# Gated delta stage: another order in its prologue, rotary angles moved into its last head, last head's output on VectorE

## The reference, cut to what matters

```python
def gdn_mixer(h, w_in, w_conv, a_log, dt_bias, w_onorm, w_out):
    proj = h @ w_in
    qkv, z, beta_logit, a_logit = split(proj)          # 3 x 1024, 1024, 8, 8 columns
    qkv = silu(causal_conv(qkv, w_conv))               # 4 taps along the tokens
    q, k, v = heads(qkv)
    q = q * rsqrt(sum(q * q) + EPS) / sqrt(d)
    k = k * rsqrt(sum(k * k) + EPS)
    beta = sigmoid(beta_logit)
    g = -exp(a_log) * softplus(a_logit + dt_bias)
    o = chunk_gated_delta(q, k, v, g, beta)            # running sums of g, state over the blocks
    o = o * rsqrt(mean(o * o) + EPS) * w_onorm
    return (o * silu(z)) @ w_out

x = x + gdn_mixer(rms_norm(x, norm_w[2]), ...)
x = x + swa_mixer(rms_norm(x, norm_w[3]), positions, ...)
#   swa_mixer rotates q and k by cos/sin of  positions[..., None] * inv_freq
```

## Time and profile before

| | |
|---|---|
| median of 3 runs | 3170.13 us (3170.04 to 3171.9) |
| profiled execution: its own time | 3169.11 us |
| profiled execution: its span | 3167.1 us |
| busy in the span: PE, DVE, ACT, POOL | 2859.8, 1312.1, 1210.2, 978.9 us |
| mean granted TensorE clock | 0.962 of full speed |
| prologue of gdn, from cb's last matmul to head 0's first | 592.1 to 632.0 us |
| gdn heads | 632.0 to 1000.9 us |
| output product of gdn, from the held parts to the last sum | 1008.9 to 1049.4 us |

### The profile page before, as it was taken

The page is one execution under the profiler, slowest core; times in us unless marked ns, Lnnn a source line. Parts: engine busy times, 40 slices in busy tenths (PEclk is TensorE's granted clock), DMA queues, the critical chain, the costliest instruction groups (busy, mean ns, idle before and its releaser), DMA issues.

```text
span 3167.1 us, 41439 instructions
## 1 busy us (share of the span) xinstructions
PE 2859.8 (90%) x13752; PEld 2148.3 (68%) x13752; DVE 1312.1 (41%) x2370; ACT 1210.2 (38%) x1832; POOL 978.9 (31%) x420
## 2 busy tenths in 40 slices
PE   6999999799998799788888999997799999899996
PEld 5777777567766577566676888875445646688875
DVE  2234223676675565555534122125543343411131
ACT  4333333344443354444443233344333333432233
POOL 3443332222232323222222444432111212344433
PEclk9999999899999899899999999999899999999998
DMA  4232221211111212211122333221100102233322
GB/s 137 92 93 79 67 66 53 67 54 39 41 53 37 70 60 63 64 53 53 54 62 64 102 97 98 94 87 56 40 27 27 60 26 60 67 93 100 93 80 67
DMA packets 59505, 213.35 MB, mean 67 GB/s; under 512 B 6560, under 2 KB 6944, under 8 KB 59296
## 3 DMA queue, kind: packets, MB, share of 16 engines
q1 hardware_dynamic: 57920, 208.46, 21.5%
q0 software_dynamic: 528, 2.10, 0.2%
q10 hardware_dynamic: 976, 1.70, 0.2%
HBM read 210.14 MB, written 2.10 MB: 67 GB/s over the span
## 4 chain that ended last, share of the span: by engine, by line
issue 53%; PE 24%; POOL 15%; DVE 6%; ACT 1%; POOLq 0%; DVEq 0%; ACTq 0%; PEldq 0%
POOL weights_low L342 15%; PE bank L386 4%; PE bank L387 4%; PE bank L388 4%; PE bank L986 3%; PE bank L988 2%; PE bank L987 2%; DVE work L1438 1%; PE bank L1083 1%; DVE work L1435 1%; DVE mixed L1945 1%; PE bank L449 0%; PE bank L1067 0%; DVE residual L1949 0%; DVE work L1508 0%
## 5 line engine op out<-in xcount | busy, mean ns | idle before, releaser
L342 POOL TENSOR_TENSOR weights_low<-weights_raw,weights_high 128x1024 fp32r<-128x1024 f32 x391 | 946.8, 2424 | 2002.7 <-ACT weights_high L335 2002.6
L386 PE MATMUL bank<-activations_high,weights_high 128*128 128x512 f32 x1848 | 729.4, 395 | 23.5 <-DVEq L2669 6.4
L387 PE MATMUL bank<-activations_low,weights_high 128*128 128x512 f32 x1848 | 721.5, 390 | 0.0
L388 PE MATMUL bank<-activations_high,weights_low 128*128 128x512 f32 x1848 | 720.9, 390 | 0.0
L986 PE MATMUL bank<-activations_high,weights_high 128*128 128x512 f32 x1232 | 534.6, 434 | 49.6 <-DVE activations_low L416 42.6
L335 ACT ACTIVATE weights_high<-weights_raw 128x1024 fp32r<-128x1024 f32 x391 | 412.1, 1054 | 352.8 <-PE bank L388 270.4
L988 PE MATMUL bank<-activations_high,weights_low 128*128 128x512 f32 x1232 | 493.1, 400 | 0.0
L987 PE MATMUL bank<-activations_low,weights_high 128*128 128x512 f32 x1232 | 493.0, 400 | 0.0
L386 PEld LDWEIGHTS bank<-activations_high,weights_high 128*128 128x128 f32 x1848 | 348.3, 188 | 109.0 <-issue 22.6
L387 PEld LDWEIGHTS bank<-activations_low,weights_high 128*128 128x128 f32 x1848 | 348.2, 188 | 74.8 <-issue 3.4
L388 PEld LDWEIGHTS bank<-activations_high,weights_low 128*128 128x128 f32 x1848 | 348.1, 188 | 73.3
(11 more groups left out here) (380 smaller groups left out, 3121.9 us busy)
## 6 DMA issues: line engine op xcount, KB each, us to landing
weights_raw<-weights SPq DMA_DIRECT2D x391, 512.0 KB, 3.6
residual<-x_t POOLq DMA_DIRECT2D x1, 2048.0 KB, 16.2
out_t<-residual SPq DMA_DIRECT2D x1, 2048.0 KB, 7.1
const<-consts SPq DMA_DIRECT2D x1, 1033.5 KB, 4.9
work<-p_t ACTq DMA_DIRECT2D x2, 512.0 KB, 3.6
work<-positions ACTq DMA_DIRECT2D x1, 256.0 KB, 3.2
root<-positions ACTq DMA_DIRECT2D x1, 256.0 KB, 3.0
param<-params SPq DMA_DIRECT2D x1, 140.5 KB, 5.0
```

Of the source, the lines that this page charges most:

```text
L342: K.nc.gpsimd.tensor_tensor(K.w_lo[:, s, :], K.raw[:, s, :], K.w_hi[:, s, :].bitcast(F32), ALU.subtract).then_inc(K.job_sems["low"], 1)
L386: K.nc.tensor.matmul(dst, wh, K.act_hi[:, t, :], start=first, stop=False)
L387: K.nc.tensor.matmul(dst, wh, K.act_lo[:, t, :], start=False, stop=False)
L388: ins = K.nc.tensor.matmul(dst, wl, K.act_hi[:, t, :], start=False, stop=last)
```

## The change

The diff has three parts.

1. Prologue. DVE's clearing moves ahead of the normalization (`gdn_cleared` tells ACT that the gates' buffer is clear). Beta is made by ACT as exp(-ln(1 + exp(-x))) and DVE's reciprocal goes. ACT's table load and `fetch` calls move between the gate steps, and the convolutions of q and k are woven into DVE's gate steps. PE does 3 parts of c0+2, the transposes, the other 5 parts, and puts 4 parts of c0+3 behind each `norm_sum`; it waits for `gdn_begin` after them. The weight splits of c0+3 to c0+5 move with them on ACT, and so on POOL.
2. Angles. The positions are loaded into `K.root` before the last head (`fetch_positions` on ACT's queue), and `rope_angles` takes the place of the empty generator in DVE's last head. The output product then uses the looped `out_residual_dve` without them. The sines stay where they were.
3. Last head's output. DVE does the three operations that POOL did, for the last head alone.

```diff
@@ gdn_pe
-    for r in range(1, 3):
-        job(e, c0 + r)
+    job(e, c0 + 1)
+    values = job_parts(e, c0 + 2)
+    take(values, 3)
     e.eng.wait_ge(K.sem("gdn_gates"), 1)
...
     ins.then_inc(K.sem("gdn_gates_t"), 1)
-    e.eng.wait_ge(K.sem("gdn_begin"), 1)
+    take(values, DT)
...
+    gate = job_parts(e, c0 + 3)
     for part in range(2):
         norm_sum(part, 0, c0 + part)
-    job(e, c0 + 3)
+        take(gate, 4)
+    e.eng.wait_ge(K.sem("gdn_begin"), 1)
@@ gdn_act   (the old gate steps and the loop of fetches are removed)
+    weight_high(e, cb + AHEAD)
+    nc.scalar.preload_act_table_set("natural_log_exp_and_others")
+    st.step(act(b.ea[32:40, 0:1], K.col("gdn_a_log", 0)[32:40, :], ACT.Exp))
+    job_wait(e, cb)
+    beta = b.gates[0:H8, :]
+    e.eng.wait_ge(K.sem("gdn_cleared"), 1)
+    step(act(beta, bank_of(e, cb)[0:H8, :], ACT.Exp, scale=-1.0))
+    step(act(beta, beta, ACT.Ln, bias=one[0:H8, :]))
+    act(beta, beta, ACT.Exp, scale=-1.0).then_inc(K.sem("gdn_beta"), 1)
+    fetch(0)
+    e.eng.wait_ge(K.sem("gdn_dt"), 1)
+    step(act(b.eg[32:40, :], b.eg[32:40, :], ACT.Exp))
+    act(b.eg[32:40, :], b.eg[32:40, :], ACT.Ln, bias=one[32:40, :]).then_inc(K.sem("gdn_ln"), 1)
+    weight_high(e, c0 + AHEAD)
+    fetch(1)
+    e.eng.wait_ge(K.sem("gdn_gates"), 1)
+    act(b.eg[32:40, :], b.bg[32:40, :], ACT.Exp).then_inc(K.sem("gdn_eg"), 1)
+    e.eng.wait_ge(K.sem("gdn_tok_in"), 1)
+    act(b.f1, b.tok[:, :, 32:40], ACT.Exp).then_inc(K.sem("gdn_f1_e"), 1)
+    weight_high(e, c0 + 1 + AHEAD)
+    silu(0)
+    fetch(2)
+    weight_high(e, c0 + 2 + AHEAD)
+    silu(1)
     roots()
...
+    fetch_positions(e, K.positions, 0)
     head(H8 - 1, False, False)
@@ gdn_pool
             weight_low(e, c0 + 3 + AHEAD + r, i)
+        if not more:
+            return
@@ gdn_dve
+    (memsets of u, sf, row2, tmp and gates, then sem_inc gdn_cleared)
     prenorm_dve(e, "gdn", "norm_w", 2 * DT, cb)
...
+    first = convolutions(0, (0, 1))
+    job_wait(e, cb)
+    (three steps on x, the second of them to gdn_dt)
+    e.eng.wait_ge(K.sem("gdn_beta"), 1)
+    release(e, cb)
+    st.step(v.memset(b.row1.bitcast(F32), 0.0))
+    take(first, 4)
+    e.eng.wait_ge(K.sem("gdn_ln"), 1)
+    (add, scale, running sum, copy to gdn_gates; three copies of rows)
+    e.eng.wait_ge(K.sem("gdn_gates_t"), 1)
+    v.tensor_copy(b.tok, by_chunk(K.ps[4][:, 0:NG * CH])).then_inc(K.sem("gdn_tok_in"), 1)
+    take(first, 4)
+    (two subtractions; after gdn_eg two copies and a subtraction; after gdn_f1_e the product f1)
     select(0)
-    take(convolutions(0, (0, 1)), 8)
     normalize()
...
-        conv_v, conv = convolutions(i, (2,)), convolutions(i + 1, (0, 1)) if more else iter(())
+        conv_v, conv = convolutions(i, (2,)), convolutions(i + 1, (0, 1)) if more else swa_angles(e)
...
+    e.eng.sem_inc(K.sem("position_room"), 1)
     head(H8 - 1, False)
+    last, split = H8 - 1, FIRST_SPLIT["gdn_y"] + H8
+    e.eng.wait_ge(K.sem("gdn_o_rstd"), H8)
+    e.eng.wait_ge(K.sem("gdn_o_free"), H8 + 1)
+    step(v.tensor_tensor(b.o, b.o, b.r, ALU.mult))
+    e.eng.wait_ge(K.sem("gdn_z"), H8)
+    v.tensor_tensor(b.o, b.o, b.z, ALU.mult).then_inc(K.sem("y_done"), 1)
+    e.eng.wait_ge(K.sem("split_high_done"), split)
+    v.tensor_tensor(K.act_lo[:, last + DT, :], b.o, K.act_hi[:, last + DT, :].bitcast(F32),
+                    ALU.subtract).then_inc(K.sem("split_done"), 1)
@@ swa
-    e.eng.wait_ge(K.sem("position_room"), 1)
-    e.eng.dma_start(b.ints, K.positions.broadcast_to([P, S])).then_inc(K.sem("position"), 16)
+    e.eng.wait_ge(K.sem("mask_room"), 1)
...
+def swa_angles(e):
+    K, b = e.K, swa_buffers(e.K)
+    return rope_angles(e, "swa_freq", b.cos, b.sin, 0, K.root[:, :].bitcast(I32), K.y[:, 0, :], K.y[:, 1, :])
...
-    e.eng.sem_inc(e.K.sem("position_room"), 1)
-    out_residual_dve(e, "gdn_out", rope_angles(e, "swa_freq", b.cos, b.sin, 0, b.ints, b.q, b.qr))
+    e.eng.sem_inc(e.K.sem("mask_room"), 1)
+    out_residual_dve(e, "gdn_out")
```

More of the change, by code:

```diff
@@ L1270, in y_high @@
         act(at(K.act_hi, i + DT), b.o, ACT.Copy).then_inc(K.sem("split_high_done"), 1)
-    for r in range(3):
-        weight_high(e, c0 + r + AHEAD)
-        fetch(r)
-    for part in range(2):
-        silu(part)
+    weight_high(e, cb + AHEAD)
[22 more added lines that the diff above has]
+    silu(1)
     roots()
@@ L1361, in gdn_dve @@
     cb = FIRST_JOB["gdn_ba"]
+    gates, tmp, gated = b.gates, b.tmp, slice(32, 40)
+    st.step(v.memset(b.u[:, :, 0:3], 0.0))
+    st.step(v.memset(b.sf, 0.0))
+    st.step(v.memset(b.row2.bitcast(F32), 0.0))
+    st.step(v.memset(tmp[gated, :], 1.0))
+    st.step(v.memset(gates[0:CH, :], 0.0))
+    st.wait()
+    e.eng.sem_inc(K.sem("gdn_cleared"), 1)
+    st.step(v.memset(by_block(tmp)[gated, :, 0:1], 0.0))
     prenorm_dve(e, "gdn", "norm_w", 2 * DT, cb)
@@ L1366, in step @@
         st.wait()
-    gates, tmp, gated = b.gates, b.tmp, slice(32, 40)
-    st.step(v.memset(b.u[:, :, 0:3], 0.0))
-    st.step(v.memset(b.sf, 0.0))
-    st.step(v.memset(b.row1.bitcast(F32), 0.0))
-    st.step(v.memset(b.row2.bitcast(F32), 0.0))
-    st.step(v.memset(tmp[gated, :], 1.0))
-    st.wait()
-    step(v.memset(by_block(tmp)[gated, :, 0:1], 0.0))
-    e.eng.wait_ge(K.sem("gdn_beta_e"), 1)
-    st.step(v.tensor_scalar(b.bg[0:H8, :], b.bg[0:H8, :], 1.0, None, ALU.add))
-    st.step(v.memset(gates[0:CH, :], 0.0))
@@ L1379, in gdn_dve @@
-    st.wait()
-    st.step(v.reciprocal(gates[0:H8, :], b.bg[0:H8, :]))
-    x, eg, g = b.r[gated, :], b.eg[gated, :], gates[gated, :]
-    st.step(v.tensor_scalar(x, bank_of(e, cb)[gated, :], K.col("gdn_dt_bias", 0)[gated, :], None, ALU.add))
-    st.wait()
-    release(e, cb)
-    v.scalar_tensor_tensor(eg, x, -1.0, x, ALU.mult, ALU.min).then_inc(K.sem("gdn_dt"), 1)
-    e.eng.wait_ge(K.sem("gdn_dt"), 1)
-    st.step(v.tensor_scalar(x, x, 0.0, None, ALU.max))
-    st.wait()
-    e.eng.wait_ge(K.sem("gdn_ln"), 1)
@@ L1391, in gdn_dve @@
-    st.step(v.tensor_tensor(x, x, eg, ALU.add))
-    st.wait()
-    st.step(v.tensor_scalar(x, x, b.ea[gated, 0:1], -1.0, ALU.mult, ALU.mult))
-    st.wait()
-    step(v.tensor_tensor_scan(g, tmp[gated, :], x, 0.0, ALU.mult, ALU.add))
-    v.tensor_copy(b.bg[0:CH, :], gates[0:CH, :]).then_inc(K.sem("gdn_gates"), 1)
-    st.step(v.tensor_copy(b.row1[0:H8, :], gates[0:H8, :]))
-    st.step(v.tensor_copy(b.part[gated, :], g))
-    st.step(v.tensor_copy(b.row1[64:72, :], g))
-    st.wait()
-    st.step(v.tensor_tensor(b.row1[32:40, :], gates[0:H8, :], b.row1[0:H8, :].bitcast(F32), ALU.subtract))
@@ L1413, in gdn_dve @@
-    st.step(v.tensor_tensor(b.f1, b.f1, b.tok[:, :, 0:H8], ALU.mult))
-    st.wait()
-    e.eng.sem_inc(K.sem("gdn_begin"), 1)
-    ring.begin()
-    e.eng.sem_inc(K.sem("gdn_o_free"), 1)
     n_sel = const_at("gdn_sel")
```

53 lines of the change are left out of this document (29 added, 24 removed).

## The result

The changed kernel takes 3145.98 us, median of 6 runs (3144.32 to 3146.61); the kernel before took 3170.01 beside it (6 runs, 3169.36 to 3171.9). The ratio is 0.9923, 95% interval 0.9911 to 0.9936: 24.0 us faster, where 25.1 and a time of 3145.0 were forecast. The profiled execution took 3145.88 with a span of 3144.0; the forecast for it was 3144.0.

A forecast was written before the change was run, and what follows sets the result against it. Bounds: the prologue's chain, with PE idle 15.94 us, and DVE with the angles in the output product. 16.0 - 2.0 + 9.3 + 1.8 = 25.1 us gives 3144.0 profiled, 3145.0 median; range 3139 to 3152.

The forecast's parts named there:

- The prologue: Layer's start up to head 0: PE, DVE and ACT arrive together, head 0 begins at 616.0, 16.0 us earlier.
- The clearing: DVE's memsets ahead of the normalization: covered by its 2.66 us wait for the root, taken as 0, uncovered up to 0.3.
- The collisions: Prologue, DVE operations beside POOL's splits: first convolution's last tap takes 2.0, second convolution ends 609.7 (hidden), a subtraction +1.8.
- a prologue of 18 us: Prologue: if a tap under way holds POOL off, by the skill's rule, the chain comes out near 18 us.
- no collision: Rival for the prologue: POOL starts a moment later or is the one held off, no collision on the path, 3143; chance 0.10.
- The low clock: Rival for the prologue: both jobs and the first sum run at 1.2 GHz, head 0 at 619, 3148; chance 0.16.
- Angles in the last head: Last head: 15 angle operations in DVE's gaps make the copy at 992.39 come 2.0 us later.
- the three gaps: DVE's waits for PE in the last head: first 0.6 late, second 0.5 late, third 3.8 of work against 2.26.
- The output product: Fifth job's start to last add: without angles 22.2 us as in fox, against 31.5, so 9.3 earlier; bounds 8.5 to 9.7.
- The last output on DVE: Last head's three output operations on DVE instead of POOL: 2.9 instead of 4.7, 1.8 us earlier; bounds 1.5 to 2.0.
- Slower: Rival: head 0 enters and stays at the low level of the clock, costing up to 43 us, 3188; chance 0.02.
- loss by order: Rival: ACT late at each hand-over, prologue gives 12 and last head costs 4, 6 us less, 3151; chance 0.09.

The follow-up runs named there:

- two splits late: The changed kernel with ACT's weight splits of c0+4 and c0+5 one step later each: 3144.42 us, ratio 0.9917 to the kernel before.
- split later: The changed kernel with the weight split of c0+3 moved behind ACT's exponential of the gates: 3146.2 us, ratio 0.9922 to the kernel before.
- values first: The changed kernel with all eight parts of c0+2 ahead of PE's transposes: 3146.16 us, ratio 0.9924 to the kernel before.

## Why the prediction was right

What bounded the old kernel was read rightly: a chain of gates, convolutions and squares in the prologue, and DVE under the angles in the output product.

**The prologue, 16.0 forecast, 14.65 measured: the one mis-sized term.** Gates, the end of DVE's copy, at 603.26 (forecast 602.9), transposes at 603.41 (begin 603.1, end 603.5), first sum 608.90 (608.7), second 612.55 (612.4), head 0's line on PE 616.58 (616.0). That last is 0.6 of the error. 0.2 of it lies ahead of c0+1, where PE's program is unchanged. The rest is on DVE: its third collision took 2.0, not 1.8, and hit a cast instead of a subtraction, so the product f1 ended at 615.29 (615.0), and the selected rows were ready at 616.42 (615.8), for DVE idles 0.55 before their first cast. The other 0.8 is the normalization. The text held it to be as long as head 0's own first products and filler need. It isn't: before, the first read followed PE's line by 0.43 us (632.42 behind 631.99); now 1.29 us of normalization stands in between on DVE, and PE waits 0.80 for the squares at 619.01. I had counted to PE's first line and not to DVE's first read, which is what head 0 hangs on.

**The clearing** was taken at nothing. It ended at 577.84, and the first scaled operation began at 577.91: the cover was just enough, and from the root to that operation 0.04 was lost.

**The collisions.** The three that I counted came, at 2.1, 2.1 and 2.0 us, and the undone weaving and the moved splits showed that they go with the splits: without one beside them three taps take 2.33. The gates wait behind the first. The second was called hidden, and for ACT it was: it found the taps done at 610.84. But DVE works from 594.63 to 616.4 with one pause of 0.55 us, so all that lengthens it is on the path; with the second and third out of its way (*two splits late*) head 0 came 1.3 earlier, with a collision of 1.55 on another cast, and then ACT was last.

The durations say how such a pair shares. The operation that is in front keeps its time, and the other is longer by the rest of it, less 0.1 to 0.2 us: in *two splits late* the cast of 128x128 that began at 610.61, under a split that lasted from 609.92 to 612.31, took 1.78 instead of 0.23. Where a split begins during a DVE operation, as in the changed kernel at 611.01 during a subtraction that runs from 610.70 to 611.38, the split has 2.61 instead of 2.39, and the *next* DVE operation pays. The Trainium skill ("SBUF — State Buffer", Who interferes with whom) gives the pair to the one that issues first and blocks the other for the whole instruction; these rows agree. My step from that rule to a prologue of 18 us was false: that subtraction held POOL up by 0.2 us only, and the operation behind it then met the split. In *split later*, where the second and third splits began during taps, each had a tap of 2.75 beside it all the same. So the rival *no collision* did not come true, and going first would not have brought it.

**The low clock** rival was half right. The low level did come, behind a pause of 2.95 us: the five parts took 5.1 us (603.77 to 608.90) where 15 matmuls at 0.227 make 3.4. But ACT's square was not there before 608.76, so only 0.14 of it reached the first sum. That it cost so little is luck: the sum had no term for it, and the 1.6 us that it had between the parts' end (607.0) and ACT's square (608.6), not meant for the clock, took it up. Where the pause was moved to a place without slack, in *values first*, it cost 1.5.

**Angles in the last head**, +1.71 for a forecast of 2.0: the three gaps filled as worked out, and the third overflowed. With the overflow taken out of it the stretch went back to 30.27. So the third gap cost 1.46, close to the 1.54 (3.8 less 2.26) of the sum, and the lateness brought into it 0.25 instead of 0.5. **The output product**, -9.33 for -9.3: DVE's last wait is PE's, as in fox, and the four sums of squares beside splits (1.18 to 1.36 us instead of 0.69) were hidden, so the angles were the bound. That it hit to 0.03 is luck: by the clock it could have been 7.7, as in seven of eleven profiles, which is outside the 8.5 to 9.7 given for it. **The last output on DVE**, -1.90 for -1.8. **Slower** and **loss by order** found nothing: head 0 stays at full clock and the heads keep their 47 us.

```profile
617.80:664.80 47.00, 42.92 (x354) 32.49 (x353) 31.31 (x63) 20.53 (x32) 10.48 (x5) 1.00 0.15 46
```

This is head 0 of the changed kernel, beside the earlier trace rows: the clock column shows 1.00 in both.

The working so missed by 0.9 in the changed stages (24.2 instead of 25.1), and another 1.0 was lost by the untouched rest in the profiled execution: 3145.88 where 3144.0 was forecast. The median, 3145.98, is only 1.0 above the forecast of 3145.0, because the runs lie 0.1 above the profiled one here, and not 1.0. That this offset took half of the miss is luck.

## What to carry to other kernels

Count a moved step to the first instruction on the engine that the next stage hangs on, not to the first instruction of that stage. Work that shares SBUF with another engine's long operations should be placed by laying both timelines over each other: moving such an operation within a busy stretch only changes its victim, and three in a row cost as much as three apart. Before a difference of one or two microseconds is laid to an edit, count it from the first instruction that the edit can touch. When a pause can't be removed, put work with slack right behind it, so that the clock's low level falls on that.

## What the runs showed of the hardware

- A GpSimd weight split of 2.4 us lengthens one DVE operation on SBUF by up to 2.2 us, whatever its size: a 128x512 tap (0.75 to 2.89), an 8x512 cast (0.42 to 2.42), an 8x512 running sum (1.21 to 3.30), a 128x128 cast (0.23 to 2.41).
- A pause of 2.95 us ahead of the transposes was followed by the low level in all five profiles that have it; pauses of 0.82 and 1.00 us in the same place, in four profiles, were not. A like pause elsewhere did not decide it: the sum over partitions took 1.94 us behind 2.77 us in one kernel and 1.13 behind 2.77 in another, and head 0 began at full level behind 3.35 us and at the low one behind 3.32.
- The output product's low stretch lay in one of two places from program to program, worth 1.6 us of 22.2. From the layer's root to the first matmul of c0+1, the same program of PE took from 16.12 to 17.17 us, by how many of its matmuls ran at the low level.
